# Memory attention inside the gated linear attention stage: each head's value products put ahead of the next level's scores

## The reference, cut to what matters

```
q, k, v, g, lr, mq = split_cols(xn @ gla_w_in[i], GLA_SIZES)
main = gla_mixer(...)                      # GLA, 4 heads, key width 96, value width 192
mo = mem_attention(mq, mem_kv)             # 4 heads of width 64 over 256 memory positions
h = h + concatenate([main, mo]) @ w_out[i]

def mem_attention(q, mem_kv):
    s = jnp.einsum('bshd,bmhd->bhsm', qh, kh).astype(jnp.float32) * MEM_HEAD_DIM ** -0.5
    p = jax.nn.softmax(s, axis=-1)
    o = jnp.einsum('bhsm,bmhd->bshd', p, vh.astype(jnp.float32))
```

## Time and profile before

| what | value |
|---|---|
| median of 3 runs | 1762.53 us (1761.74 to 1764.82) |
| the profiled execution's own time | 1762.53 us |
| its span, first to last instruction | 1760.7 us |
| PE busy | 1584.7 us, 90% of the span |
| PEld busy | 1136.0 us, 65% |
| DVE busy | 740.7 us, 42% |
| ACT busy | 398.7 us, 23% |
| POOL busy | 285.3 us, 16% |
| mean granted TensorE clock | 0.986 |

### The profile page before, as it was taken

The page is one execution under the profiler, slowest core; times in us unless marked ns, Lnnn a source line. Parts: engine busy times, 40 slices in busy tenths (PEclk is TensorE's granted clock), DMA queues, the critical chain, the costliest instruction groups (busy, mean ns, idle before and its releaser), DMA issues. The chain is left out here.

```text
span 1760.7 us, 18212 instructions
## 1 busy us (share of the span) xinstructions
PE 1584.7 (90%) x6374; PEld 1136.0 (65%) x6378; DVE 740.7 (42%) x1946; ACT 398.7 (23%) x944; POOL 285.3 (16%) x285
## 2 busy tenths in 40 slices
PE   7999989899777777777779999999989999999997
PEld 6888865454223333223257788888878877888886
DVE  2102565677667767675525432211231134322113
ACT  1110122222222222222134311111113134211111
POOL 0000033334434434443203001000000000000000
PEclk9999999999999999999989999999999999999999
DMA  6443399999999999999923145344324310433440
GB/s 256 154 157 124 107 394 424 426 426 420 427 426 427 427 427 420 423 422 416 403 99 109 65 161 199 143 160 162 143 75 140 105 42 1 180 143 143 158 163 24
DMA packets 56164, 419.14 MB, mean 238 GB/s; under 512 B 6372, under 2 KB 6692, under 8 KB 10048
## 3 DMA queue, kind: packets, MB, share of 16 engines
q0 software_dynamic: 38240, 274.83, 37.5%
q1 hardware_dynamic: 17856, 143.46, 22.2%
HBM read 416.19 MB, written 1.09 MB: 237 GB/s over the span
## 5 line engine op out<-in xcount | busy, mean ns | idle before, releaser
L1453 PE MATMUL wide<-arena 128*128 128x512 f32 x1024 | 477.1, 613 | 117.3 <-ACT arena L459 116.9
L1292 PE MATMUL bank<-hT,wring 128*128 128x256 f32 (+2 forms) x2512 | 556.5, 381 | 15.7 <-DVE hT L825 15.7
L1292 PEld LDWEIGHTS bank<-hT,wring 128*128 128x128 f32 (+2 forms) x2512 | 470.2, 188 | 93.2 <-issue 17.2
L1453 PEld LDWEIGHTS wide<-arena 128*128 128x128 f32 x1024 | 190.0, 193 | 392.8 <-issue 196.2
L967 DVE CUSTOM_DVE_ANT_0 arena<-arena,wide 128x1024 f32<-128x1024 f32 x256 | 312.6, 1221 | 193.4 <-DMA arena<-uv_dram,arena 193.1
L413 POOL DMA_INDIRECT arena<-uv_dram,arena x256 | 257.1, 1004 | 480.9 <-PE wide L1453 285.7
L1137 DVE SCALAR_TENSOR_TENSOR arena<-bank,prm,arena 128x254 f32<-128x254 f32 (+1 forms) x176 | 76.8, 478 | 339.1 <-ACT arena L459 333.1
L459 ACT ACTIVATE arena<-arena 128x2 f32<-128x2 f32 (+3 forms) x196 | 66.9, 343 | 525.4 <-DVE arena L967 439.1
L1630 PE MATMUL wide<-arena,wring 128*128 128x256 f32 x704 | 159.3, 379 | 1.2 <-DVE arena L1151 1.2
L1630 PEld LDWEIGHTS wide<-arena,wring 128*128 128x128 f32 x704 | 133.6, 190 | 20.1 <-DVE arena L1151 2.0
L459 ACT ACTIVATE arena<-bank,prm 128x256 f32<-128x256 f32 (+1 forms) x96 | 48.2, 552 | 318.3 <-PE bank L1292 317.2
(11 more groups left out here) (190 smaller groups left out, 1125.1 us busy)
## 6 DMA issues: line engine op xcount, KB each, us to landing
wring<-ffn_dram SPq DMA_DIRECT2D x44, 1536.0 KB
wring<-win_dram SPq DMA_DIRECT2D x16, 1024.0 KB
wring<-wout_dram SPq DMA_DIRECT2D x8, 1024.0 KB
wring<-wout_dram SPq DMA_DIRECT2D x4, 1280.0 KB
wring<-mix_dram SPq DMA_DIRECT2D x4, 1024.0 KB
wring<-wqd_dram SPq DMA_DIRECT2D x4, 1024.0 KB
arena<-uv_dram,arena POOLq DMA_INDIRECT x256
wring<-memkv_dram SPq DMA_DIRECT2D x4, 1024.0 KB
```

Source lines behind the costliest of these rows:

```text
L1292: ins = MM(b[0:rows, m * S:(m + 1) * S], w[:, (m * kt + k) * width:(m * kt + k) * width + rows], src[:, k, :], start=k == 0, stop=k == kt - 1)
L1453: ins = MM(wide[:, 2 + h, :], diag[:, n % 4, e, :], G[:, r % NBUF, D + 512 * h:D + 512 * (h + 1)], start=r % (HEADS * TOPK) == 0, stop=r % ...
```

## The change

Two streams are written in another order; no instruction is added, removed or altered. On ACT, `summed(J)` follows `turned(J)` at once (the new helper `outs(J)`), where it used to stand further back. On PE, `values(0)`, `values(1)`, `values(2)` and `values(3)` each move ahead of the `pair` that they used to follow. DVE, POOL and SP have the same streams as before.

```diff
+            def outs(J):
+                turned(J)
+                summed(J)
...
             decay(4)
-            turned(0)
+            outs(0)
             expo(2)
             decay(5)
-            summed(0)
-            turned(1)
+            outs(1)
             expo(3)
             decay(6)
-            summed(1)
             keep_v(2)
-            turned(2)
+            outs(2)
             decay(7)
-            summed(2)
-            turned(3)
-            summed(3)
+            outs(3)
...
             turn(0)
             score(2)
+            values(0)
             pair(3)
-            values(0)
             turn(1)
             score(3)
+            values(1)
             pair(4)
-            values(1)
             gla_v(2)
             turn(2)
+            values(2)
             pair(5)
-            values(2)
             turn(3)
+            values(3)
             pair(6)
-            values(3)
             gla_v(3)
```

## The result

The changed kernel takes 1773.66 us (median of 6 runs, 1770.03 to 1774.81) against 1762.68 us before (6 runs): slower, ratio 1.0055 with a 95% interval of 1.0045 to 1.0066. By the ratio that is 9.7 us (7.9 to 11.6; the two medians lie 11.0 apart); I had said 5.3. The median lies above the top of my range, 1770.5 us. The profiled execution has a span of 1773.0 us, 12.3 more than before.

The account below looks back on a forecast made before the run. The stretch was taken as bound by PE, at two points by a loop through DVE; shifts of 2.5 to 2.6, 0 (-0.1), 1.8 to 1.9 and 0.9 to 1.0, taken as 5.3 us, gave 1767.8 us, range 1765.8 to 1770.5.

Parts of the forecast that it names:

- Place 1: values(0) ahead of pair(3): a 1.67 us hole on PE waiting for turned(0); turn(1) 2.5 to 2.6 us later.
- Place 3: values(2) ahead of pair(5): a 0.86 us hole on PE, and pair(5) starts later; 1.8 us, up to 1.9.
- Place 4: values(3) ahead of pair(6): a 0.86 us hole on PE and 0.05 us of restart; 0.9 us, up to 1.0.
- ACT's order: On ACT, earlier summed copies and later expo and decay passes hold up nothing: 0 us.
- The loop through DVE: pair(3) feeds keep_pairs(3), probs(1) stands behind, turn(1) needs it; likewise pair(5) to turn(3): 3.69 to 3.78 us.
- Everything behind `gla_v(3)` shifts along: From gla_v(3) PE has no gap until far behind the stage, so its 5.3 us shift moves the kernel's end.
- swallowed: Rival: behind the stage, a PE wait for a weight transfer absorbs the 5.3 us, leaving 1762.5 us; chance 0.06.
- the clock falls on top: Rival: PE's clock falls once to 1.2 GHz in the changed stretch, adding 2.7 us, 1770.5 us; chance 0.17.

Follow-up runs that it names:

- all waits filled: Changed kernel with useless matmuls on PE at its waits (7, 7, 3, 7, 3 before values and turn items): 1769.3 us against 1764.23 before.
- ACT's order alone: Kernel before with only ACT's stream reordered as in the change, PE's stream as before: 1764.17 us against 1764.23.
- PE's order alone: Kernel before with only PE's stream reordered as in the change, ACT's stream as before: 1773.53 us against 1764.23.
- `probs` early: Changed kernel with probs(1) ahead of keep_pairs(3) and probs(3) ahead of keep_pairs(5) on DVE: 1765.45 us against 1763.13 before.
- fillers before `turn`: Changed kernel with 7 useless matmuls each before turn(1) and turn(3) only, waits before values left empty: 1768.16 us against 1763.05 before.
- the fastest version: Kernel before with probs(1), probs(3) moved ahead on DVE and useless matmuls at PE's long waits elsewhere: 1754.71 us against 1763.05, ratio 0.9948.

## Why the prediction was wrong

- **Place 1, 2.5 to 2.6 us: right.** With the clock whole, `turn(2)` is 2.55 us later (from the start of `score(2)`: 16.98 us with all waits filled, 14.43 before). The parts too: a wait of 1.59 us before `values(0)` (about 1.6 forecast), one of 1.72 before `turn(1)` (1.7), none before `values(1)`.
- **Place 3, 1.8 us: right.** `turn(2)` to `turn(3)` takes 5.95 us against 4.13, +1.82, in the changed kernel itself.
- **Place 4, 0.9 us: right by itself** (`turn(3)` to `gla_v(3)` 4.12 us filled, 3.17 before, +0.95), but 2.46 us in the changed kernel, as it carries a fall.
- **ACT's order, 0: right**, shown by the run of ACT's order alone.
- **The loop through DVE: right**, shown by taking it away in both kernels.
- **"Everything behind `gla_v(3)` shifts along": consistent.** The waits of PE behind the stage are the same five groups of the same size to 0.1 us; nothing was swallowed. What the profile has on top there, 1.3 us, goes with the fall at 1524 to 1532 us shown above, which belongs to the execution and not to the change. The ratio's 9.7 us and the stage's 10.06 agree within the interval.
- **The clock: this is the step that failed.** I had it as a rival, "the clock falls on top", with a chance of 0.17, once, for 2.7 us. It fell in each of the two profiles of the changed kernel, three times, for 1.5 to 1.6 us each: 3.2 us up to `turn(2)` (5.78 against 2.55 of shift) and 1.5 us behind `turn(3)` (2.46 against 0.95), 4.7 us together. The sum, 10.0 us, is what was measured.

The argument that misled me was "against it: the work between the two waits is longer here, and the second pair of holes is shorter". It had no number behind it. What the rows did show was one instance for the fall and an example against it with gaps of 0.84 us; my waits of 1.6 and 1.7 us lay at the first, not at the second. I also priced one fall, and not one for each wait of that length: there were three. The rule of the Trainium skill that I quoted ("TensorE: Matmul & The Clock Gate", "A second HAM failure mode: psum-queue depth-cycling") would have led to the right outcome: short standstills of PE between groups made the clock swing, three times in the stage. But they need not come often: here a single one of 1.6 to 1.7 us was enough.

Still open: in which execution a given wait brings the clock down. With the same waits of PE the first place had two short falls in the changed kernel and one long one in PE's order alone; with only the wait before `values(0)` left it had one (`probs` early) or none (fillers before `turn`). Counted over the nine profiles that have such waits, PE stood for 1.59 to 1.73 us without fillers 17 times in the stage, and a low stretch followed right behind 13 of them; behind the waits of 0.16 to 0.84 us alone there was none. I did not vary the length of a single wait, and can't say from which length on it happens.

## What to carry to other kernels

Moving a consumer directly behind its producer can cost twice on PE: the wait itself, and then the work behind it at half clock. When a sum opens new waits of PE like the ones here (1.6 to 1.7 us) on the critical path, put a fall of the clock for each such wait (1.3 to 1.6 us here for a short one) into the forecast, not into the tail. And where PE must wait anyway, matmuls of no use that end just before the wait does can pay: here they took 4.7 us off a stage and, placed at the old gaps and together with the move of `probs`, 9 us off the kernel.

## What the runs showed of the hardware that was not expected

- A low stretch in the stage was short (each of the three in the changed kernel fits into 3.7 to 3.8 us) or about twice as long (977.6 to 984.9 us with PE's order alone). It went on while PE worked without a gap: PE was busy for 3.80 of 3.80, 3.70 of 3.70 and 7.30 of 7.30 us; only the third one of the changed kernel (3.35 of 3.80) has a gap in it.
- Two profiles of the changed kernel, of executions of the same length, agree to 0.02 us at every item of the stage, low stretches included.
- A fall came where PE had no waits: in the fastest version PE ran 36-column matmuls without a gap and the clock was low right behind them. The timeline of PE and the stretch, of that version:

```profile
1329.24 4.12 PE L1669 MATMUL bank<-wring,arena 128*128 128x36 f32 x32
1333.30 2.09 PE L1531 MATMUL wide<-memk,arena 64*128 64x256 f32 x8
```

```profile
1333.00:1339.50 6.50, 6.50 (x16) 3.31 (x17) 1.92 (x6) 1.20 (x3) 0.00 (x0) 0.53 0.61 231
```

What the cause is there was not tried.
